# Second mixer of a two-block network: heads in pairs, keys in three stages, f32 sums

## The chip, the core and the metric

The program runs on one core of one Trainium2 chip. The metric is the device time of one execution in microseconds (us), the median of a few runs. The engines are called PE (TensorE), DVE (VectorE), ACT (ScalarE), POOL (GpSimd) and SP (SyncE, which issues the DMAs). PSUM has eight banks here, `ps0` to `ps7`, of 128 x 512 f32.

## What is computed

Ten stages on 512 tokens of width 1024: six of a first block (four gated FFNs, a recurrent mixer, a stick-breaking attention mixer) and four of a second block. The change touches only the stick-breaking mixer, the fifth stage:

```python
def stick_breaking_mixer(h, w_qkv, w_out):
    q, k, v = jnp.split(h @ w_qkv, 3, axis=-1)      # 16 heads of 64
    for s0 in range(0, seqlen, Q_BLOCK):
        end = s0 + Q_BLOCK
        ...
        z = jnp.einsum("bqhd,bkhd->bhqk", qb, kb).astype(jnp.float32) * scale
        mask = k_pos[None, :] < q_pos[:, None]
        log_1m = jnp.where(mask, jax.nn.log_sigmoid(-z), 0.0)
        between = lax.cumsum(log_1m, axis=3, reverse=True) - log_1m
        att = jnp.where(mask, jnp.exp(jax.nn.log_sigmoid(z) + between), 0.0)
        outs.append(jnp.einsum("bhqk,bkhd->bqhd", att.astype(vb.dtype), vb))
    ...
    return o @ w_out
```

With softplus(z) = -log_sigmoid(-z) this is att = exp(z - sum of softplus(z) over this key and all later ones), for keys before the query.

## The kernel before

**Layout.** Activations lie with features on partitions and the 512 tokens along the free axis. A weight block of 128 x 128 arrives by DMA in chunks of eight (`RAW`), is split by ACT into a rounded high half (`SPH`, type fp32r) and by DVE into the rest (`SPL`), and every projection is three fp32r matmuls per block (L740 to L742). Chunks are split a few ahead of PE (`halve_to`). Each engine runs its own list of instructions in the order in which it is written, with waits on counting semaphores; a planner (`Ring.plan`) gives each tile its PSUM bank and tells what must have ended before.

**The mixer** (`mix1` in each engine's program). Q and K are projected into `WK` units 0 to 7 and 8 to 15 (unit = 512 columns, two heads in one unit, head h on partitions 64*(h%2) up), V by tokens into units 16 to 23 (L780 to L782, copied out by ACT at L1586). Then 16 heads, one after the other. For a head the scores are made with keys on partitions, in four tiles of 128 keys, `kt` = 3, 2, 1, 0, with 512 - 128*kt queries each (128, 256, 384, 512 columns; 1280 in all):

- PE `scores` (L1095): four f32 matmuls with 64 rows, into PSUM.
- DVE `start_tile`: x = max(z, 0) (L2224), y = z - 2x (L2226); ACT: exp (L1604), ln(1 + .) (L1606); DVE `end_tile` (L2231): the negated softplus; POOL (L2605) zeroes the masked triangle with an affine select; ACT (L1611) rounds to fp32r (`LMH`), POOL (L2616) subtracts for the low half (`LML`).
- PE `weights` (L1111): for each key tile the suffix sum, as matmuls with a triangle (`SUF`) or `ONES` over this and all later tiles, once for the high and once for the low half, added onto the scores in PSUM: 2 x 2560 columns of fp32r a head.
- ACT (L1628): exp out of PSUM into `AT`; POOL (L2605) zeroes the triangle again.
- PE `values` (L1122): four f32 matmuls with 64 columns into bank `ob`, shared by two heads. ACT (L1634) and DVE (L2250) make the high and low half of the pair's output in `HH`, `HL`.

PE's order is `weights(h)`, `scores(h+1)`, `values(h)`. Then the output projection `project_out` (64 blocks; output tile m over its 8 inputs k, m after m), squares by ACT, copies and a running sum of squares by DVE (`squares_of_out`, `copies_of_out`), the sums over rows (L802, L804), a normalisation and the next stage.

Of the kernel before, what the change touches and what calls it, by code (L numbers as in the profile page):

```python
# [59 lines left out]
def constants():  # L60
# [16 lines left out]
    c["suffix"] = (i >= t)  # L77
    c["ones"] = np.ones((128, 128))
# [141 lines left out]
EARLY_OUT = {1: [4, 5, 6, 7]}  # L220
# [25 lines left out]
def build(nc, a, order, known):  # L246

    ctx = ExitStack()
    with ctx:
# [80 lines left out]
        def al(m):  # L330
            return AL[:, m * T:(m + 1) * T]
# [39 lines left out]
        def u8(x, rows=slice(0, 128), first=0, n=32):  # L371
# [5 lines left out]
        stick = {"LMH": [AL[:, u * T:u * T + 1280] for u in (3, 6)], "LML": [AL[:, u * T:u * T + 1280] for u in (9, 12)],  # L377
                 "AT": [WK[:, u * T:u * T + 1280] for u in (37, 40)]}
# [36 lines left out]
        def out_of(s):  # L415

            return Yh if s in NAMES or s in (CONV0, CONV1) else Y0 if s == MIX0 else Ya
# [162 lines left out]
        def plan_mix1():  # L580
            s = MIX1
            plan_first(s, "proj", lambda i: ("qk", i))
            ps.plan(("xsum", s), ("xln", s))
            ps.plan(("rcolp",), ("rcln",))
            for i in range(6, 16):
                ps.plan(("proj", s, i), ("qk", i))
                plan_chunk(BASE[s] + i)
            for half in range(2):
                for c in range(4):
                    ps.plan(("vp", s, half, c), ("v", half, c))  # L590

            def scores(h):
                for kt in (3, 1, 0):
                    ps.plan(("z", h, kt), ("att", h, 2 if kt == 3 else kt))
                for kt in (3, 1, 0):
                    scr.plan(("zx", h, kt), ("zl", h, 2 if kt == 3 else kt))
                    scr.plan(("zy", h, kt), ("lo", h, 2 if kt == 3 else kt))
            scores(0)
            for h in range(16):
                if h < 15:  # L600
                    scores(h + 1)
                if h % 2 == 0:
                    ps.plan(("ob", h // 2), ("al1", h // 2), hold=True)
                else:
                    ps.release(("ob", h // 2))
            plan_postnorm(s, BASE[s] + 24, 8)
# [105 lines left out]
        def tensor_program(e):  # L712
# [355 lines left out]
            def mix1(s):  # L1068
# [8 lines left out]
                for i in range(6, 16):  # L1077
                    project(s, i, "l1_w_qkv", cols[i])
                for half in range(2):
                    project_tokens(s, half, 512, "l1_w_qkv", 2048 + 512 * half)  # L1080
                off = [0, 512, 896, 1152]
                SO = al(21)[:, 0:256]
                SUF, ONES = SO[:, 0:128], SO[:, 128:256]

                def zof(h, kt):
                    b = ps["z", h, 3 if kt == 2 else kt]
                    return b[:, 256:384] if kt == 3 else b[:, 0:512 - 128 * kt]

                def scores(h):
                    m, p0 = h // 2, 64 * (h % 2)  # L1090
                    w.wait_ge(("qk", m), ("qk", 8 + m))
                    for kt in range(3, -1, -1):
                        if kt != 2:
                            w.wait_ge(*ps.before("z", h, kt))
                        e.matmul(zof(h, kt), wk(8 + m)[p0:p0 + 64, 128 * kt:128 * kt + 128],  # L1095
                                 wk(m)[p0:p0 + 64, 128 * kt:T], start=kt != 2, stop=False,
                                 skip_group_check=True).then_inc(pe_done.did(("z", h, kt)))

                def weights(h):
                    lh, ll = stick["LMH"][h % 2], stick["LML"][h % 2]  # L1100
                    w.wait_ge(("suf",))
                    for kt in range(3, -1, -1):
                        w.wait_ge(("lo", h, kt))
                        if kt == 3:
                            w.wait_ge(("zneg", h, 2))
                        for half in (lh, ll):
                            for jt in range(3, kt - 1, -1):
                                nj, oj = 512 - 128 * jt, off[jt]
                                sh = 128 * (jt - kt) + (256 if kt == 3 else 0)
                                b = ps["z", h, 3 if kt == 2 else kt]  # L1110
                                mm = e.matmul(b[:, sh:sh + nj], SUF if jt == kt else ONES, half[:, oj:oj + nj],  # L1111
                                              start=False, stop=half is ll and jt == kt, skip_group_check=True)
                        mm.then_inc(pe_done.did(("sum", h, kt)))

                def values(h):
                    p0, at = 64 * (h % 2), stick["AT"][h % 2]
                    if h % 2 == 0:
                        w.wait_ge(*ps.before("ob", h // 2))
                    w.wait_ge(("cut", h, 0), ("v", 1, 3))
                    for kt in range(4):  # L1120
                        n, o = 512 - 128 * kt, off[kt]
                        mm = e.matmul(ps["ob", h // 2][p0:p0 + 64, 128 * kt:T], wk(16 + 2 * kt, 2)[:, 64 * h:64 * h + 64],  # L1122
                                      at[:, o:o + n], start=kt == 0, stop=kt == 3, skip_group_check=True)
                    mm.then_inc(pe_done.did(("val", h)))
                scores(0)
                for h in range(16):
                    weights(h)
                    if h < 15:
                        scores(h + 1)
                    values(h)  # L1130
                project_out(s, "l1_w_out", 8, hp, lambda k: ("al1", k))
# [188 lines left out]
        def scalar_program(e):  # L1320
# [254 lines left out]
            def mix1(s):  # L1575
# [3 lines left out]
                rsqrt_of(ps["rcolp",][:, 0:4], rcol, EPS6, 1.0, ("rcln",), ("rcol",))  # L1579
                for i in range(6, 16):  # L1580
                    halve_to(ahead_of(s, i))
                for half in range(2):
# [5 lines left out]
                w.wait_ge(("sufl",))  # L1588
                e.activation(al(21)[:, 0:256], wk(24)[:, 0:256], ACT.Copy).then_inc(act_done.did(("suf",)))
                off = [0, 512, 896, 1152]  # L1590
                ln_exp_table()

                def zy(h, kt):
                    q = 256 if kt == 3 else 0
                    return scr["zy", h, 3 if kt == 2 else kt][:, q:q + 512 - 128 * kt]

                def zof(h, kt):
                    b = ps["z", h, 3 if kt == 2 else kt]
                    return b[:, 256:384] if kt == 3 else b[:, 0:512 - 128 * kt]

                def start_tile(h, kt):
                    y = zy(h, kt)
                    w.wait_ge(("zneg", h, kt))
                    e.activation(y, y, ACT.Exp).then_inc(act_done.did(("zexp", h, kt)))  # L1604
                    w.wait_ge(("zexp", h, kt))
# [1250 lines left out]
```

## Time and profile before

| | us |
|---|---|
| median of 3 runs | 3832.0 (3827.67 to 3833.7) |
| the profiled execution | 3837.11 |
| its span in the trace | 3835.4 |
| busy PE / DVE / ACT / POOL | 3588.8 / 1944.1 / 1399.8 / 99.8 |
| the mixer's heads in the trace, from the last V projection to the first matmul of the output projection | about 1725 to 1979.8 |

The page gives each engine's busy time, the 40 slices with the clock that PE was granted, and the chain of work that ended last. In the slices PE is at nine tenths almost everywhere at a granted clock of 0.9 to 1.0 of full speed, and in slices 19 and 20 the granted clock is 0.6 and 0.7, POOL is busy for the only time and the DMAs rest: that is the mixer. A full granted clock (1.00) is 2.4 GHz, 0.50 is 1.2 GHz. An f32 matmul stands in the trace as two records (one for each pass over the columns; together a column takes about four times as long as one of fp32r), an fp32r one as one. Rates are therefore read from the starts of matmuls that follow each other; the length of one record holds some 0.17 us until its result is seen.

### The profile page before, as it was taken

To read this page: it belongs to the slowest core of one execution; us is meant where nothing else is said; L and a number is where in the kernel's file an instruction comes from. 1 tells how busy PE (TensorE), PEld (TensorE's weight loads), DVE (VectorE), ACT (ScalarE), POOL (GpSimd) and SP (SyncE) were. 2 spreads that over 40 slices of the span, in tenths; PEclk is the share of its full clock that TensorE was granted. 3 is DMA by queue.
4 is the path that set the end of the run, shared out by engine and by line. 5 is a ranking of instruction groups with operands and counts; after the bars stand their busy time and mean duration, and the time that the engine had idled before them with its cause. 6 is when DMAs were issued, how large, how long until landed. Compare 5 with 4: busy or idle time off the path is not lost.

```text
span 3835.4 us, 47526 instructions
## 1 busy us (share of the span) xinstructions
PE 3588.8 (94%) x20316; PEld 2825.4 (74%) x20316; DVE 1944.1 (51%) x2753; ACT 1399.8 (36%) x2086; POOL 99.8 (3%) x210
## 2 busy tenths in 40 slices
PE   8999886899999999897889999999999999889998
PEld 6888665778887888784457888765788877668886
DVE  5554665356544643423436443646566344656652
ACT  4322453233323332325434322235444233444433
POOL 0000000000000000003320000000000000000000
PEclk9999986899999999996679999989999999899999
DMA  5444320024443432220002222310233231012231
GB/s 181 143 143 143 110 94 4 2 94 154 143 143 104 160 109 95 79 97 6 0 28 83 99 96 97 126 61 2 71 105 99 96 125 65 28 39 94 99 99 55
DMA packets 93091, 342.37 MB, mean 89 GB/s; under 512 B 10320, under 2 KB 10960, under 8 KB 92368
## 3 DMA queue, kind: packets, MB, share of 16 engines
q1 hardware_dynamic: 92880, 339.33, 26.5%
q8 instruction: 160, 2.62, 0.3%
q14 instruction: 51, 0.42, 0.0%
HBM read 337.20 MB, written 2.10 MB: 88 GB/s over the span
## 4 chain that ended last, share of the span: by engine, by line
PE 83%; ACT 7%; DVE 7%; issue 2%; POOL 2%; DMA 0%; SPq 0%; ACTq 0%; DVEq 0%
PE ps L740 20%; PE ps L741 20%; PE ps L742 20%; PE ps L757 3%; PE ps L758 3%; PE ps L761 3%; POOL AL L2616 1%; ACT WK L1778 1%; PE ps L1111 1%; PE ps L780 1%; PE ps L781 1%; PE ps L782 1%; PE ps L809 1%; ACT SPH L1330 1%; ACT L1334 1%
## 5 line engine op out<-in xcount | busy, mean ns | idle before, releaser
L1864 DVE TENSOR_TENSOR SPL<-RAW,SPH 128x1024 fp32r<-128x1024 f32 x522 | 637.1, 1224 | 1096.5 <-ACT SPH L1330 1096.4
L740 PE MATMUL ps<-HH,SPH 128*128 128x512 f32 x2416 | 959.5, 397 | 21.8 <-DVE WK L2207 7.7
L1330 ACT ACTIVATE SPH<-RAW 128x1024 fp32r<-128x1024 f32 x522 | 548.8, 1056 | 1103.2 <-PE ps L742 975.4
L741 PE MATMUL ps<-HL,SPH 128*128 128x512 f32 x2416 | 947.4, 392 | 0.0
L742 PE MATMUL ps<-HH,SPL 128*128 128x512 f32 x2416 | 946.5, 392 | 0.0
L740 PEld LDWEIGHTS ps<-HH,SPH 128*128 128x128 f32 x2416 | 458.5, 190 | 132.1 <-issue 12.5
L741 PEld LDWEIGHTS ps<-HL,SPH 128*128 128x128 f32 x2416 | 458.6, 190 | 97.6 <-issue 3.9
L742 PEld LDWEIGHTS ps<-HH,SPL 128*128 128x128 f32 x2416 | 457.9, 190 | 97.2
L740 PE MATMUL ps<-AH,SPH 128*128 128x512 f32 x1088 | 423.8, 390 | 0.0
L742 PE MATMUL ps<-AH,SPL 128*128 128x512 f32 x1088 | 423.3, 389 | 0.0
L741 PE MATMUL ps<-AL,SPH 128*128 128x512 f32 x1056 | 410.8, 389 | 0.0
L757 PE MATMUL ps<-HH,SPH 128*128 128x512 f32 x480 | 200.6, 418 | 55.2 <-ACT HH L1370 25.0
L742 PEld LDWEIGHTS ps<-AH,SPL 128*128 128x128 f32 x1088 | 204.2, 188 | 42.6
L740 PEld LDWEIGHTS ps<-AH,SPH 128*128 128x128 f32 x1088 | 204.3, 188 | 42.0
L741 PEld LDWEIGHTS ps<-AL,SPH 128*128 128x128 f32 x1056 | 198.3, 188 | 41.1
L758 PE MATMUL ps<-HH,SPL 128*128 128x512 f32 x480 | 197.9, 412 | 0.0
L757 PEld LDWEIGHTS ps<-HH,SPH 128*128 128x128 f32 x480 | 97.4, 203 | 83.6 <-ACT HH L1370 29.1
L761 PE MATMUL ps<-HL,SPH 128*128 128x512 f32 x480 | 122.2, 390 | 0.0
L1111 PE MATMUL ps<-AL 128*128 128x128 f32 (+2 forms) x320 | 77.3, 390 | 45.7 <-POOL AL L2616 45.6
L1392 ACT ACTIVATE SCR<-SCR 128x512 f32<-128x512 f32 x88 | 55.8, 634 | 169.3 <-DVE SCR L1935 169.3
L758 PEld LDWEIGHTS ps<-HH,SPL 128*128 128x128 f32 x480 | 97.6, 203 | 20.9
L1851 DVE SCALAR_TENSOR_TENSOR ADA<-RAW,PCT,ADA 128x1024 f32<-128x1024 f32 x84 | 107.4, 1279 | 0.0
(416 smaller groups left out, 3900.7 us busy)
## 6 DMA issues: line engine op xcount, KB each, us to landing
RAW<-in_ws SPq DMA_DIRECT2D x522, 512.0 KB, 3.3
RAW<-in_wa SPq DMA_DIRECT2D x96, 512.0 KB, 3.3
WK<-in_sm SPq DMA_DIRECT2D x2, 2784.0 KB, 9.7
WK<-in_cst SPq DMA_DIRECT2D x2, 1664.0 KB, 7.4
X<-in_x SPq DMA_DIRECT2D x8, 256.0 KB, 7.7
out<-X SPq DMA_DIRECT2D x8, 256.0 KB, 2.1
WK<-in_sm SPq DMA_DIRECT2D x1, 768.0 KB, 5.1
WK<-in_cst SPq DMA_DIRECT2D x3, 128.0 KB, 2.4
```

Source lines behind the costliest of these rows:

```text
L740: e.matmul(out, wh, rhs[0], start=start, stop=False)
L741: e.matmul(out, wh, rhs[1], start=False, stop=False)
L742: mm = e.matmul(out, wl, rhs[0], start=False, stop=stop)
L757: e.matmul(ps["proj", s, i][:], wh, hh, start=k == 0, stop=False)
L758: e.matmul(ps["proj", s, i][:], wl, hh, start=False, stop=False)
L761: mm = e.matmul(ps["proj", s, i][:], wh, hl, start=False, stop=k == 7)
L780: e.matmul(o, hh, wh[:, 0:n], start=k == 0, stop=False)
L1111: mm = e.matmul(b[:, sh:sh + nj], SUF if jt == kt else ONES, half[:, oj:oj + nj], start=False, stop=half is ll and jt == kt, skip_group_ch ...
L1330: e.activation(SPH[:, q:q + 1024], RAW[:, r:r + 1024], ACT.Copy).then_inc(hi_ready.did(("hi", n)))
L1392: e.activation(scr["g", s, m], scr["g", s, m], ACT.Silu).then_inc(act_done.did(("silu", s, m)))
L1851: e.scalar_tensor_tensor(ADA[:], raw, c, ADA[:], ALU.mult, ALU.add).then_inc(dve_done.did(("ada", i)))
L1864: e.tensor_tensor(SPL[:, q:q + 1024], RAW[:, r:r + 1024], SPH[:, q:q + 1024].bitcast(F32), ALU.subtract).then_inc(lo_ready.did(("lo", n)))
```

## The change

- Two heads go together (a pair, m = 0 to 7), and the keys of a pair go in three stages: `STAGES` 0: tiles kt 2 and 3 (384 columns a head in one bank), 1: kt 1 (384), 2: kt 0 (512). That is 24 steps n = 3m + stage. Each step has a bank for each head (`zs`, six banks, so three steps), outputs alternate over banks 6 and 7.
- PE writes the scores of the two heads alternately (partitions 0 to 63 and 64 to 127), and the values alternately (output partitions 0 to 63 and 64 to 127).
- The masks are added in PSUM: after the scores one fp32r matmul of 128 columns per key tile and head, identity times a triangle of -1e30 (`IR`, `CA`, made by ACT at the start of the mixer from a constant that is loaded with the others). POOL has nothing left to do in the mixer.
- Softplus is max(z, ln(1 + exp(min(z, 40)))): DVE min, ACT exp, ACT ln, DVE max, each on 384 or 512 columns of a head, in buffers `SP`.
- The suffix sums are f32 matmuls of `SP` itself (2560 columns a head, no halves), with negated triangle and ones. The order of keys within a step changes which of them are one matmul.
- PE's order is scores(n+2), sums(n), values(n-1). scores(0) stands ahead of the V projections.
- The pair's output goes over Q and K of that pair (`AH` units m and 8+m), the copies of the output projection over V (`Y1`).
- `EARLY_OUT` for this stage: output tiles 0 to 3 first take inputs 0 to 6, then input 7 for the four; then tiles 4 to 7 alike. The chunks are split up to other numbers ahead (`ahead_of_out`).

```diff
-EARLY_OUT = {1: [4, 5, 6, 7]}
+EARLY_OUT = {1: [4, 5, 6, 7], 4: [0, 1, 2, 3, 4, 5, 6]}
...
+        STAGES = [((2, 0), (3, 256)), ((1, 0),), ((0, 0),)]
+        WIDTH, AT_SP = [384, 384, 512], [0, 384, 768]
...
+            zs, outs = (0, 1, 4, 5, 2, 3), (6, 7)
+
+            def scores(n):
+                for h in range(2):
+                    ps.plan(("z", n, h), ("att", n, h), group=zs)
...
+                def scores(n):
+
+                    m, tiles = n // 3, STAGES[n % 3]
+                    w.wait_ge(("qk", m), ("qk", 8 + m), ("masks1",), *ps.before("z", n, 0), *ps.before("z", n, 1))
+                    for kt, o in tiles:
+                        for h in range(2):
+                            p0 = 64 * h
+                            e.matmul(ps["z", n, h][:, o:o + 512 - 128 * kt],
+                                     wk(8 + m)[p0:p0 + 64, 128 * kt:128 * kt + 128], wk(m)[p0:p0 + 64, 128 * kt:T],
+                                     start=o == 0, stop=False, skip_group_check=True)
+                    for kt, o in tiles:
+                        for h in range(2):
+                            mm = e.matmul(ps["z", n, h][:, o:o + 128], IR, CA, start=False, stop=False,
+                                          skip_group_check=True)
+                    mm.then_inc(pe_done.did(("z", n)))
...
+                    for h in range(2):
+                        z, sp = ps["z", n, h], SP[m % 2][h]
+                        w.wait_ge(("sp", n, h))
+                        e.matmul(z[:, 0:WIDTH[st]], SUF, sp[:, AT_SP[st]:AT_SP[st] + WIDTH[st]], start=False, stop=False,
+                                 skip_group_check=True)
...
+                        for x, o in later:
+                            mm = e.matmul(o, ONES, x, start=False, stop=True, skip_group_check=True)
+                        mm.then_inc(pe_done.did(("sum", n, h)))
...
+                scores(1)
+                for n in range(24):
+                    if 0 < n < 22:
+                        scores(n + 2)
+                    sums(n)
+                    if n == 0:
+                        scores(2)
+                    else:
+                        values(n - 1)
+                values(23)
+                project_out(s, "l1_w_out", 8, lambda k: (ah(k), ah(8 + k)), lambda k: ("al1", k))
...
+                def logs(n):
+                    for h in range(2):
+                        w.wait_ge(("min", n, h))
+                        e.activation(part(n, h), part(n, h), ACT.Exp).then_inc(act_done.did(("exp", n, h)))
+                    for h in range(2):
+                        w.wait_ge(("exp", n, h))
+                        e.activation(part(n, h), part(n, h), ACT.Ln, bias=ONE).then_inc(act_done.did(("ln", n, h)))
...
+                for n in range(24):
+                    if n == 0:
+                        weights(0)
+                    if n < 22:
+                        logs(n + 2)
+                    if n:
+                        weights(n)
+                    if n and n % 3 == 0:
+                        out_hi(n // 3 - 1)
...
+                low(0)
+                high(0)
                 halve_to(BASE[s] + 23 + AHEAD)
...
+                low(1)
+                for n in range(24):
+                    if n < 22:
+                        low(n + 2)
+                    if n < 23:
+                        high(n + 1)
+                    if n > 1 and n % 3 == 1:
+                        out_lo(n // 3 - 1)
+                out_lo(7)
```

**PE, one head before.** The list of PE between the scores of head 0 and the first sums of head 1 (`AL` holds the halves of the softplus, `WK` Q, K, V and the weights):

```order
L1111 MATMUL ps<-AL 128x128 [waits s_gpsimd_done]
L1111 MATMUL ps<-AL 128x256
L1111 MATMUL ps<-AL 128x384
L1111 MATMUL ps<-AL 128x512
L1111 MATMUL ps<-AL 128x128
L1111 MATMUL ps<-AL 128x256
L1111 MATMUL ps<-AL 128x384
L1111 MATMUL ps<-AL 128x512
L1095 MATMUL ps<-WK 128x128
L1095 MATMUL ps<-WK 128x256
L1095 MATMUL ps<-WK 128x384
L1095 MATMUL ps<-WK 128x512
```

The sums of each key tile wait for POOL; the scores of the next head come behind them.

**PE, one step now.** The same engine in the steps n = 2 and 3 (L1096 scores, L1101 masks, L1112 and L1122 sums, L1133 values):

```order
L1096 MATMUL ps<-WK 128x512 [waits s_scalar_done]
L1096 MATMUL ps<-WK 128x512
L1101 MATMUL ps<-AL 128x128 x2
L1112 MATMUL ps<-WK 128x384 [waits s_vector_done]
L1122 MATMUL ps<-WK 128x128
L1112 MATMUL ps<-WK 128x384 [waits s_vector_done]
L1122 MATMUL ps<-WK 128x128
L1133 MATMUL ps<-WK 64x512 x2
```

Scores moved two steps ahead of the sums that use them; what they wait for is now ACT, whose exponentials free the banks of the step before.

**ACT, one head before:**

```order
L1628 ACTIVATE WK<-ps 128x128 [waits s_tensor_done]
L1628 ACTIVATE WK<-ps 128x256
L1628 ACTIVATE WK<-ps 128x384 [waits s_tensor_done]
L1628 ACTIVATE WK<-ps 128x512 [waits s_tensor_done]
L1604 ACTIVATE SCR<-SCR 128x128 [waits s_vector_done]
L1606 ACTIVATE SCR<-SCR,SML 128x128 [waits s_scalar_done]
L1604 ACTIVATE SCR<-SCR 128x256 [waits s_vector_done]
L1606 ACTIVATE SCR<-SCR,SML 128x256 [waits s_scalar_done]
```

**ACT, two steps now** (L1614 exp, L1617 ln, L1622 the weights, L1627 the high half of a pair's output):

```order
L1614 ACTIVATE WK<-WK 128x512 [waits s_vector_done] x2
L1617 ACTIVATE WK<-WK,SML 128x512 [waits s_scalar_done] x2
L1622 ACTIVATE WK<-ps 128x384 [waits s_tensor_done] x2
L1627 ACTIVATE AH<-ps 128x512 [waits s_tensor_done]
L1614 ACTIVATE WK<-WK 128x384 [waits s_vector_done] x2
L1617 ACTIVATE WK<-WK,SML 128x384 [waits s_scalar_done] x2
L1622 ACTIVATE WK<-ps 128x384 [waits s_tensor_done] x2
```

The exponentials of a step now stand behind the logarithms of the step two further on; the rounding copies (L1611) are gone.

## Rows read from the trace of the kernel before

**Rows 1.** Stretch, length; busy us of PE, PEld, DVE, ACT, POOL; granted clock; DMA.

```profile
1900.00:1950.00 50.00, 43.23 (x113) 22.38 (x112) 21.18 (x44) 24.93 (x55) 19.11 (x39) 0.64 0.00 1
```

**Rows 2.** The chain that ended last, one head: start us, us, what.

```profile
1877.85 1.27 POOL AL L2616
1879.16 2.71 PE ps L1111 x8
...
1893.53 1.28 POOL AL L2616
```

**Rows 3.** Waits from 1733 to 1985 us: us in total, times, longest.

```profile
DVE SCR L2224 <- PE ps L1095: 99.9, 15, 9.1
...
PE ps L1111 <- POOL AL L2616: 45.6, 41, 6.9
```

**Rows 4.** The same mixer stretches finer, split where the granted clock changes.

```profile
1864.87:1875.11 10.24, 10.24 (x21) 4.64 (x19) 5.66 (x12) 5.23 (x11) 2.67 (x6) 0.50 0.00 1
1875.11:1878.52 3.41, 2.06 (x13) 1.57 (x12) 0.00 (x0) 1.92 (x5) 2.02 (x4) 1.00 0.00 0
```

**Rows 5.** PE in a later stage, 2641 to 2651 us: paired f32 matmuls and masks at clock 1.00.

```profile
2641.39 2.09 PE L1272 MATMUL ps<-WK 128*64 128x512 f32 x12
...
2644.37 1.13 PE L1244 MATMUL ps<-WK 64*128 64x512 f32 x4
2645.43 0.44 PE L1248 MATMUL ps<-AL 128*128 128x128 f32 x2
...
2647.27 1.14 PE L1244 MATMUL ps<-WK 64*128 64x384 f32 x8
2648.33 0.66 PE L1248 MATMUL ps<-AL 128*128 128x128 f32 x4
...
2650.00 0.70 PE L1244 MATMUL ps<-WK 64*128 64x256 f32 x4
2650.64 0.44 PE L1248 MATMUL ps<-AL 128*128 128x128 f32 x2
```

**Rows 6.** PE at the end of the output projection: last block, then f32 sums.

```profile
2023.67 0.39 PE L742 MATMUL ps<-HH,SPL 128*128 128x512 f32 x1
2023.90 1.02 PE L802 MATMUL ps<-ACC,CST 128*128 128x512 f32 x2
...
2024.76 1.12 PE L804 MATMUL ps<-SCR,CST 128*128 128x512 f32 x2
```

**Rows 7.** PE at clock 0.50: one f32 matmul of 512 columns, two records.

```profile
1884.53 1.91 PE L1095 MATMUL ps<-WK 64*128 64x512 f32 x2
```

**Rows 8.** Groups by line and shape, 1733 to 1985 us: busy us, mean ns of one.

```profile
L1606 ACT ACTIVATE SCR<-SCR,SML 128x512 f32<-128x512 f32 x16 | 11.6, 722 | 0.5
...
L1628 ACT ACTIVATE WK<-ps 128x384 f32<-128x384 f32 x16 | 7.9, 495 | 0.7 <-PE ps L1111 0.6
...
L2224 DVE TENSOR_SCALAR SCR<-ps 128x512 f32<-128x512 f32 x16 | 10.9, 684 | 0.0
...
L2224 DVE TENSOR_SCALAR SCR<-ps 128x384 f32<-128x384 f32 x15 | 8.3, 551 | 0.0
L1604 ACT ACTIVATE SCR<-SCR 128x384 f32<-128x384 f32 x15 | 7.9, 524 | 6.1 <-DVE SCR L2226 6.1
```

**Rows 9.** The chain again: four copies of V, and the first output matmul.

```profile
1726.25 2.31 ACT WK L1586 x4
...
1979.76 0.73 PE ps L740
```

**Rows 10.** The later stage again, by stretches, with PE's granted clock.

```profile
2640.00:2660.00 20.00, 18.55 (x121) 10.17 (x121) 15.21 (x40) 12.22 (x39) 0.00 (x0) 1.00 0.00 1
```

**Rows 11.** DVE in the last 5 us of the output projection: start us, us.

```profile
2019.29 0.69 DVE L1905 TENSOR_TENSOR ACC<-ACC,SCR 128x512 f32<-128x512 f32 x1 [3.02 <-ACT SCR L1356]
...
2019.89 0.69 DVE L1907 COPY Ya<-ps 128x512 f32<-128x512 f32 x1
...
2020.50 1.22 DVE L1864 TENSOR_TENSOR SPL<-RAW,SPH 128x1024 fp32r<-128x1024 f32 x1
```

More of the change, by code:

```diff
@@ L75, in constants @@
     c["diag"] = i32 == j32
-    c["suffix"] = (i >= t)
-    c["ones"] = np.ones((128, 128))
+    c["suffix"] = -1.0 * (i >= t)
+    c["ones"] = -np.ones((128, 128))
+    c["later"] = np.where(i < t, 0.0, -1e30)
     pm = np.zeros((128, 128))
@@ new lines, in values @@
+                def values(n):
+                    m, tiles = n // 3, STAGES[n % 3]
+                    if n % 3 == 0:
+                        w.wait_ge(*ps.before("ob", m))
+                    w.wait_ge(("att", n, 0), ("att", n, 1), ("v", 1, 3))
+                    for kt, o in tiles:
+                        for h in range(2):
+                            p0 = 64 * h
+                            mm = e.matmul(ps["ob", m][p0:p0 + 64, 128 * kt:T],
+                                          wk(16 + 2 * kt, 2)[:, 64 * (2 * m + h):64 * (2 * m + h) + 64],
+                                          AT[n % 4][h][:, o:o + 512 - 128 * kt], start=kt == 2, stop=kt == 0,
+                                          skip_group_check=True)
+                    mm.then_inc(pe_done.did(("val", n)))
@@ L1079, in mix1 @@
+                scores(0)
                 for half in range(2):
                     project_tokens(s, half, 512, "l1_w_qkv", 2048 + 512 * half)
[L1081 to L1131, printed above, removed]
+                scores(1)
+                for n in range(24):
+                    if 0 < n < 22:
+                        scores(n + 2)
+                    sums(n)
+                    if n == 0:
+                        scores(2)
+                    else:
+                        values(n - 1)
@@ L1631, in values @@
-                def values(h):
-                    if h % 2:
-                        w.wait_ge(("val", h), ("vp", s, 1, 3))
-                        e.activation(hp(h // 2)[0], ps["ob", h // 2][:], ACT.Copy).then_inc(
-                            act_done.did(("ah1", h // 2)))
-                scores(0)
-                for h in range(16):
-                    weights(h)
-                    if h < 15:
-                        scores(h + 1)
-                    values(h)
+                logs(1)
@@ L2243, in mix1, with part @@
[L2243 to L2251 removed]
+                SP = stick["SP"]
+                def part(n, h):
+                    o = AT_SP[n % 3]
+                    return SP[n // 3 % 2][h][:, o:o + WIDTH[n % 3]]
@@ new lines, in low, with high @@
+                def low(n):
+                    w.wait_ge(("z", n))
+                    for h in range(2):
+                        w.wait_ge(*([("sum", n - 4 - n % 3, h)] if n >= 6 else ah_free(s)))
+                        e.tensor_scalar(part(n, h), ps["z", n, h][:, 0:WIDTH[n % 3]], 40.0, None, ALU.min).then_inc(
+                            dve_done.did(("min", n, h)))
+                def high(n):
+                    for h in range(2):
+                        w.wait_ge(("ln", n, h))
+                        e.tensor_tensor(part(n, h), ps["z", n, h][:, 0:WIDTH[n % 3]], part(n, h), ALU.max).then_inc(
+                            dve_done.did(("sp", n, h)))
```

180 lines of the change are left out of this document (49 added, 131 removed).

## The prediction

> **What bounds the kernel now.** I read the slices first: PE is busy nearly everywhere and the clock is full nearly everywhere, except in the mixer. So the mixer is where time can come from, and the rest (projections at one fp32r matmul after the other) is untouched by the change. Then the mixer by stretches: in 50 us PE is "busy" 43.2, but at a granted clock of 0.64 [rows 1]. The chain shows who ends last: from one head's last POOL subtraction to the next head's is 1893.53 - 1877.85 = 15.7 us, and it runs through all engines: POOL's halves, PE's sums behind them, PE's next scores, DVE, ACT, POOL again [rows 2]. 16 heads of 15.7 are 251 us; with the start the mixer takes from about 1725, where the V projections end and ACT copies their last tiles, to 1979.8, where the output projection begins [rows 9]: 254.8 us. The waits say the same: DVE waits 9.1 us at most in a head, 99.9 in all, for the scores, because they stand behind the sums in PE's list, and PE waits 45.6 us for POOL's low halves [rows 3]. No engine has enough work for 15.7 us at full speed; the loop is a chain handed round. Its pauses also cost clock: after a stretch at 1.00 in which PE was busy 2.06 of 3.41 us the clock is at 0.50 again, where the sums, scores and values then run without a pause (10.24 of 10.24 us busy) at half rate [rows 4].
>
> **PE's work for a pair now, at the full clock.** The nearest rows for scores, masks and values are those of a later stage, which pairs its heads in the same way [rows 5].
> - Scores and masks, from the first matmul to the result in PSUM. A 512-column pair takes 2645.43 - 2644.37 = 1.06, two masks 0.44: 1.50 for stage 2. A 256-column pair takes 0.64, so 128 columns are 0.21, and 384 with two masks is 0.85 + 0.44 = 1.29 (stage 1). Stage 0, 256 and 128 with four masks, is 1.06 (for 384 and 128) - 0.21 + 0.66 = 1.51. PE is free again some 0.17 earlier each time: 4.3 us to the results, 3.8 of PE.
> - Sums: f32 of 512 columns start 0.86 apart [rows 6], 1.68 ns a column. 2 x 512, 2 x 768 and 2 x 1280 columns are 1.72, 2.58 and 4.30: 8.6 us. That is the part that gets dearer, twice what 2 x 2 x 2560 fp32r columns would cost at the same clock.
> - Values: 2.09 for 512, 384 and 128 columns, less the 0.17, and about 0.5 for 256: 2.4.
>
> Together 14.8 us a pair, against 2 x 15.7 = 31.4 now. By rows 5 a 512-column f32 pair costs 1.06 where two alone would cost 2 x 0.86, so pairing gives 1.6 times, not 2. The Trainium skill (TensorEngine Tiling (Array Packing), Theoretical Speedup and Key Properties) has up to 2 times for 64 rows, and says that changing the tiling mode drains the engine. By the 2 the scores would be 2.15 instead of 2.7 and the values 2.15 instead of 2.4, by its drain rule something in between; this case's trace has both effects in 1.06, and the sum goes by that.
>
> **ACT's work.** One exp, ln of 512 or exp out of PSUM of 384 takes 0.63 to 0.72 and 0.50 [rows 8], but four in a row of 512 take 2.31 [rows 9], 0.58 each; with 0.107 us less for 128 columns less (the 0.524 of the shorter exp) a queued one of 384 is 0.47. DVE takes 0.68 or 0.55 a tile [rows 8], and has four a step, 7.5 us a pair with the output: never the bound. POOL's affine selects and subtractions, the rounding copies and two of three DVE passes leave the chain.
>
> **The new loop, step by step.** PE's scores(n+2) wait for both exponentials of step n-1, since these free the banks. Behind them come: first min on DVE, two exps and two lns of step n+2, then two exps of step n, which free the next banks. Two paths compete:
> - by ACT: scores to result + one DVE tile + 4 ACT + 2 ACT + about 0.2 for ends and semaphores. n = 3m: 1.50 + 0.68 + 4 x 0.58 + 2 x 0.47 + 0.2 = 5.64. n = 3m+1: 1.51 + 0.55 + 6 x 0.47 + 0.2 = 5.08. n = 3m+2: 1.29 + 0.55 + 4 x 0.47 + 2 x 0.58 + 0.2 = 5.08.
> - by PE: scores + sums + 0.2 + one exp. n = 3m: 1.33 + 1.72 + 0.7 = 3.75. n = 3m+1: 1.34 + 2.58 + 0.7 = 4.62. n = 3m+2: 1.12 + 4.30 + 0.17 + 0.6 + 0.05 = 6.24.
>
> Values(n-1) go into the time in which PE waits for the exponentials. The later end counts: 5.64 + 5.08 + 6.24 = 17.0 us a pair, of which PE works 14.8. If every ACT tile takes its full single length the first two steps are 0.4 longer each: 17.8.
>
> **Start and end.** scores(0) now stand ahead of the V projections and wait for the last Q/K tile to leave bank 1 (about 1.0), and take 1.5: +2.6 with nothing beside them. Their logarithms are hidden by the V projections. After V, ACT first splits a chunk and copies the last V tiles (to +3.5 as now [rows 9]), then does two exps, two lns and the exponentials of step 0: step 1 begins at +6.4. Steps 1 and 2: 11.3. Steps 3 to 20: six pairs of 17.0, 102. From step 21: scores, sums and values 3.05 + 1.0, sums(22) and values to 7.3, sums(23) 4.30, last exp 0.8, last values 1.0: 13.5. Total 2.6 + 6.4 + 11.3 + 102 + 13.5 = 135.8 us in place of 254.8: **-119.0**.
>
> The other order of the output projection costs nothing at its start (inputs 0 to 6 are long there, banks 0 to 5 free). At its end it does: output tiles 4 to 7 end 3 matmuls of 0.227 apart, 0.68 us [rows 6], instead of 24, 5.4. Behind tile 4 stand on DVE: sum, copy, a chunk to split (1.22), sum, copy, sum at 0.6 each, where now all but one are over before the last matmul [rows 11]. DVE's last sum then comes about 3 us after PE's last matmul, where L802 now follows at once [rows 6]: **+3**. Bounds: 0, if the chunk is split earlier, and 5. ACT's mask constants, a table load and the longer DMA cost nothing: they lie beside projections.
>
> Sum: -116. For the clock I add 2 (below): -114. On the profiled execution's span 3835.4 - 114 = 3721; it lay 5 us above the median with what surrounds it, so against the median 3832.0: **3718 us**.
>
> **Rivals.**
> - *The clock still falls, once in most pairs.* In a step 3m PE pauses 5.64 - 1.33 - 1.72 - 1.0 = 1.6 us, in 3m+1 0.5. Before, a pause of 1.35 us between short bursts was followed by the low level [rows 4]; in the later stage PE is busy 18.55 of 20 us in small pieces and keeps 1.00 [rows 10]. With 1.6 in 17 us I expect it to hold, so I add only 2 us. Falling once a pair for 10.24 us [rows 4] doubles 5 us of PE work, of which the pauses take 1 to 2: 4 us a pair, 32 in all: 3750. Chance 0.21. The Trainium skill (TensorE: Matmul & The Clock Gate, Part 1) calls the low clock the default that activity lifts; by that rule a denser loop lifts itself, and the trace agrees, since the fully busy low stretch of rows 4 is followed by 1.00.
> - *The heads of a pair don't overlap*, in the sums' neighbourhood unlike in rows 5. Scores 4.3 instead of 2.7, values 4.3 instead of 2.4, a third hidden: +2.5 a pair, 20 us: 3738. Chance 0.05. Against it: same partitions and same form of instruction as in rows 5.
> - *PE at the low level for the whole mixer.* PE alone then sets the loop: 2 x 14.8 = 29.6 a pair, 237 and 12 for the ends, near 250: with the +3 no change, 3830. Chance 0.02.
> - *Slower: the same, and f32 weight loads show.* At 0.50 one f32 matmul of 512 is 1.71 between starts [rows 7], double; a pair has 36 passes of sums, many of only 128 or 256 columns, each with its own load of weights. If each shows 0.1 us of its load, a pair takes 33.2 us, the mixer 278 with its ends: +26, 3858. It decides from 31.4 - 29.6 = 1.8 us a pair, 0.05 a pass, and only without the full clock. Chance 0.03. Against it: PE would then be busy without pause, the very stretch that rows 4 show ended by 1.00.
>
> **Numbers.** Forecast 0.69: 3706 to 3728 (start and end 4 either way, 17.0 to 17.8 a pair). The range takes in the falling clock with its bounds (2 to 6 us a pair) and the serial pairs, and leaves out the last two: 3706 to 3766. A measurement of this kernel can tell about 0.2% from no change, 7.7 us. Faster 0.95, within 0.2% 0.02, slower 0.03.
>
> **What would show it.** Granted clock 1.00 in the mixer, PE about 87% busy; the scores of two heads starting together; from one pair to the next 17 us; ACT's wait for PE longest before the exponentials of stage 2, PE's wait for ACT longest ahead of the scores in steps 3m; POOL empty; L802 3 us behind the last matmul of the projection. I am wrong if a pair takes over 19 us at clock 1.00 (then an ACT or DVE tile or the sums are mis-sized), or if the clock is under 0.9.

## The result, and the profile after

The changed kernel takes 3720.4 us (median of 4 runs, 3719.26 to 3726.31), the kernel before 3829.8 (4 runs, 3824.83 to 3833.7): a ratio of 0.9718, 95% interval 0.9701 to 0.9735, 109.5 us less. The forecast was 3718, and 3706 to 3766 as its range.

In the following table the mixer stage is cut at the starts of PE's matmuls, in the two profiled executions. "Mixer" alone means, here and below, the part from the last V matmul to the first output-projection matmul.

| part of the mixer stage | before, us | after, us | difference |
|---|---|---|---|
| Q and K projections, now with scores(0) at their end | 65.3 | 67.0 | +1.7 |
| V projections | 43.3 | 47.8 | +4.5 |
| last V matmul to first output-projection matmul | 255.0 | 134.7 | -120.3 |
| output projection to L802 / L809 | 44.2 | 46.7 | +2.5 |
| from there to the next stage's first matmul | 7.0 | 8.6 | +1.6 |
| sum (of the unrounded parts) | 414.8 | 304.8 | -109.9 |

The sum agrees with the medians. The spans themselves differ by more (3835.4 and 3718.1): 4.8 us of that lie ahead of this stage and 2.6 behind it, in code that is the same in both. Where a kernel reaches this stage moves by more than that: in the 13 profiles of the changed kernel and its variants the V projections begin between 1669.5 and 1681.9 us. The kernel before, measured again beside the experiments, has medians of 3833.8, 3828.5 and 3825.9. Therefore the experiments below are read by this table first, and a difference of some 4 us between medians is not put down to an edit.

The whole mixer before and then 60 us of it after (columns as in [rows 1]):

```profile
1724.71:1979.69 254.98, 208.19 (x579) 115.23 (x577) 96.60 (x200) 123.86 (x270) 96.41 (x192) 0.65 0.01 3
```

```profile
1735.00:1795.00 60.00, 55.77 (x272) 33.36 (x270) 24.39 (x46) 33.98 (x69) 0.00 (x0) 1.00 0.00 0
```

The waits of the changed kernel from 1735 to 1860 us (us in total, times, longest):

```profile
DVE WK L2226 <- PE ps L1101: 67.9, 20, 4.7
ACT WK L1614 <- DVE WK L2226: 42.0, 20, 2.4
PEld ps L1096 <- ACT WK L1622: 19.3, 20, 2.2
ACT WK L1622 <- PE ps L1122: 14.1, 10, 2.7
...
PE ps L1096 <- ACT WK L1622: 7.9, 6, 1.3
```

The granted clock is 1.00 where its mean was 0.65, and POOL is empty. The 0.65 means that about 176 of the 255 us ran at the low level. PE's waits for POOL [rows 3] are replaced by one wait a pair of 1.3 us: the scores wait for ACT's exponentials of the step before. PE is busy 92% of the mixer. One pair on PE (start us, us):

```profile
1789.85 0.44 PE L1101 MATMUL ps<-AL 128*128 128x128 f32 x2
1790.12 1.07 PE L1112 MATMUL ps<-WK 128*128 128x512 f32 x2
1791.03 1.46 PE L1122 MATMUL ps<-WK 128*128 128x384 f32 x6
...
1794.58 0.87 PE L1133 MATMUL ps<-WK 128*64 128x384 f32 x4
1795.43 1.13 PE L1096 MATMUL ps<-WK 64*128 64x512 f32 x4
...
1798.64 1.08 PE L1133 MATMUL ps<-WK 128*64 128x512 f32 x4
1801.04 0.92 PE L1096 MATMUL ps<-WK 64*128 64x256 f32 x8 [1.31 <-ACT WK L1622]
...
1805.13 0.87 PE L1133 MATMUL ps<-WK 128*64 128x256 f32 x8
1806.07 0.92 PE L1096 MATMUL ps<-WK 64*128 64x384 f32 x4
```

The scores of the steps begin at 1795.43, 1801.04 and 1806.07, and those of the step before the first of these at 1789.00: 6.43, 5.61 and 5.03 us for n = 3m+2, 3m and 3m+1, 17.07 a pair. The idle time in brackets stands only ahead of the scores that follow a step 3m.

### The profile page after: what moved, and what is told of

It is laid out like the page before. It is cut to its first block, busy times and chain, and to the rows that moved or that the text cites. A ratio compares the mean times of both kernels' runs of the same rounds, so it can differ in the third digit from the quotient of the medians.

```text
span 3718.1 us, 47147 instructions
## 1 busy us (share of the span) xinstructions
PE 3504.7 (94%) x20348; PEld 2780.3 (75%) x20348; DVE 1902.6 (51%) x2657; ACT 1354.9 (36%) x1975; POOL 3.6 (0%) x18
## 4 chain that ended last, share of the span: by engine, by line
PE 86%; ACT 6%; DVE 5%; issue 1%; DMA 0%; SPq 0%; ACTq 0%; DVEq 0%
PE ps L747 21%; PE ps L749 20%; PE ps L748 20%; PE ps L764 3%; PE ps L765 3%; PE ps L768 3%; ACT WK L1784 1%; PE ps L787 1%; PE ps L788 1%; PE ps L789 1%; PE ps L816 1%; ACT SPH L1350 1%; PE ps L1122 1%; ACT L1354 1%; DVE SPL L1870 1%
## 5 line engine op out<-in xcount | busy, mean ns | idle before, releaser
L747 PE MATMUL ps<-HH,SPH 128*128 128x512 f32 x2352 | 933.6, 397 | 22.1 <-DVE WK L2213 8.1
L748 PE MATMUL ps<-HL,SPH 128*128 128x512 f32 x2352 | 922.3, 392 | 0.0
L749 PE MATMUL ps<-HH,SPL 128*128 128x512 f32 x2352 | 921.6, 392 | 0.0
L747 PEld LDWEIGHTS ps<-HH,SPH 128*128 128x128 f32 x2352 | 446.1, 190 | 129.2 <-issue 12.1
L748 PEld LDWEIGHTS ps<-HL,SPH 128*128 128x128 f32 x2352 | 446.0, 190 | 95.9 <-issue 3.9
L749 PEld LDWEIGHTS ps<-HH,SPL 128*128 128x128 f32 x2352 | 445.7, 189 | 94.1
L747 PE MATMUL ps<-AH,SPH 128*128 128x512 f32 x1152 | 448.9, 390 | 0.0
L749 PE MATMUL ps<-AH,SPL 128*128 128x512 f32 x1152 | 448.2, 389 | 0.0
L764 PE MATMUL ps<-HH,SPH 128*128 128x512 f32 x480 | 200.9, 419 | 55.0 <-ACT HH L1390 24.9
L747 PEld LDWEIGHTS ps<-AH,SPH 128*128 128x128 f32 x1152 | 216.2, 188 | 45.7 <-issue 0.8
L749 PEld LDWEIGHTS ps<-AH,SPL 128*128 128x128 f32 x1152 | 216.2, 188 | 45.0
L765 PE MATMUL ps<-HH,SPL 128*128 128x512 f32 x480 | 198.8, 414 | 0.0
L764 PEld LDWEIGHTS ps<-HH,SPH 128*128 128x128 f32 x480 | 97.6, 203 | 84.3 <-ACT HH L1390 29.8
L768 PE MATMUL ps<-HL,SPH 128*128 128x512 f32 x480 | 122.6, 391 | 0.0
L765 PEld LDWEIGHTS ps<-HH,SPL 128*128 128x128 f32 x480 | 97.7, 204 | 21.0
L768 PEld LDWEIGHTS ps<-HL,SPH 128*128 128x128 f32 x480 | 91.2, 190 | 19.5
```

Source lines behind the costliest of these rows:

```text
L747: e.matmul(out, wh, rhs[0], start=start, stop=False)
L748: e.matmul(out, wh, rhs[1], start=False, stop=False)
L749: mm = e.matmul(out, wl, rhs[0], start=False, stop=stop)
L764: e.matmul(ps["proj", s, i][:], wh, hh, start=k == 0, stop=False)
L765: e.matmul(ps["proj", s, i][:], wl, hh, start=False, stop=False)
L768: mm = e.matmul(ps["proj", s, i][:], wh, hl, start=False, stop=k == 7)
```

## Experiments

Each is an edit of the changed kernel, whose mixer takes 134.7 us.

### The order of the output projection

```diff
-EARLY_OUT = {1: [4, 5, 6, 7], 4: [0, 1, 2, 3, 4, 5, 6]}
+EARLY_OUT = {1: [4, 5, 6, 7]}
```

> The changed kernel, but the output projection of this mixer takes its tiles m one after the other again (EARLY_OUT without stage 4). My theory: the interleaved order costs at its end, since four output tiles finish 0.7 us apart and DVE and ACT still have three of them to do; the last sum over rows then comes 2.5 us late and runs at the low clock after the pause. Expected 4 us less than the changed kernel's 3720.4: 3716, with L809's counterpart right behind the last matmul and both sums at full clock. Rival: the end is hidden by the next stage's first loads, or the order helps at the start of the projection: 3720 or more.

Measured: 3712.0 us, ratio to the kernel before 0.9684 (0.967 to 0.9698). The two last parts of the table are 43.7 and 7.0 instead of 46.7 and 8.6: -4.7 us. The median moved by 8.4; 4.1 us of that lie ahead of this stage, where the code is the same. The end of the projection in the changed kernel:

```profile
1906.85 0.68 DVE L1911 TENSOR_TENSOR ACC<-ACC,SCR 128x512 f32<-128x512 f32 x1
...
1907.59 1.87 PE L809 MATMUL ps<-ACC,CST 128*128 128x512 f32 x2 [2.91 <-DVE ACC L1911]
1909.25 1.91 PE L811 MATMUL ps<-SCR,CST 128*128 128x512 f32 x2
```

and in this one:

```profile
1900.17 0.39 PE L749 MATMUL ps<-AH,SPL 128*128 128x512 f32 x1
1900.40 1.02 PE L809 MATMUL ps<-ACC,CST 128*128 128x512 f32 x2
```

PE's 2.91 us of waiting are DVE's sums of squares of the tiles that ended together. The two f32 sums then run at half rate (1.66 us apart in place of 0.86), where the granted clock behind the pause is the low one: the projection is 3.0 us longer than with the tiles in order, which is the wait, and the part behind it 1.6 us longer, which is the clock.

The wait is certain and the low clock behind it is not. Nine of the profiles have this pause of 2.91 us, and in three of them (V copies first, fp32r sums, no masks) the clock stayed at 1.00 while the two sums ran, and the part behind the pause took 7.0 us as without it. V copies first:

```profile
1895.07 1.13 PE L809 MATMUL ps<-ACC,CST 128*128 128x512 f32 x2 [2.91 <-DVE ACC L1913]
1896.03 1.02 PE L811 MATMUL ps<-SCR,CST 128*128 128x512 f32 x2
```

### The pause between the halves of V

```diff
-                    halve_to(BASE[s] + 16 + 4 * half + 3 + AHEAD)
+                    halve_to(BASE[s] + 16 + 4 * half + 2 + AHEAD)
                     for c in range(4):
+                        if c == 2:
+                            halve_to(BASE[s] + 16 + 4 * half + 3 + AHEAD)
```

> The changed kernel, but ACT copies two V tiles of each half before it splits the chunk that it can only split when the half is over. Theory: PE's pause of 2.6 us between the halves of the V projection, followed by a stretch at the low clock, is the wait for the PSUM banks 2 and 3, which the second half now takes over from the first and ACT frees behind its split. Expected: the pause shrinks below 1 us, the clock stays, 4 us less: 3716. Rival: PE waits for DVE's split of that chunk, as the profile's releaser says; then the split comes 1.2 us later and the time is 3721 or 3722.

Measured: 3716.4 us, 0.97 (0.9683 to 0.9717). The median moved by 4, and its four runs spread over 14 us (3708.8 to 3722.9), so it shows nothing by itself; the trace is clearer: V projections 43.4 us instead of 47.8, the other parts up to L809 within 0.4 us. (The last part was 7.0 instead of 8.6, though the edit leaves its code as it was: the sums ran at the full clock, as shown above. That is not counted for the edit.) The pause in the changed kernel, on ACT and on PE, and the clock around it (1.00, then 0.50):

```profile
1700.44 1.06 ACT L1350 ACTIVATE SPH<-RAW 128x1024 fp32r<-128x1024 f32 x1 [4.38 <-PE ps L789]
1701.40 2.40 ACT L1635 ACTIVATE WK<-ps,SML 128x512 f32<-128x512 f32 x4
...
1702.90 0.64 PE L787 MATMUL ps<-SPH,HH 128*128 128x512 f32 x1 [2.56 <-DVE SPL L1870]
```

```profile
1700.00:1703.04 3.04, 0.48 (x3) 0.17 (x2) 1.23 (x1) 2.60 (x4) 0.00 (x0) 1.00 0.00 1
1703.04:1706.46 3.42, 3.42 (x9) 2.65 (x10) 0.00 (x0) 0.76 (x2) 0.00 (x0) 0.50 0.52 157
```

and after the edit:

```profile
1690.65 1.37 ACT L1637 ACTIVATE WK<-ps,SML 128x512 f32<-128x512 f32 x2 [2.28 <-PE ps L789]
1692.75 1.06 ACT L1350 ACTIVATE SPH<-RAW 128x1024 fp32r<-128x1024 f32 x1 [0.73 <-PE ps L789]
...
1693.84 1.23 DVE L1872 TENSOR_TENSOR SPL<-RAW,SPH 128x1024 fp32r<-128x1024 f32 x1 [4.21 <-ACT SPH L1350]
```

The releaser named in the profile, DVE's split, was not what PE waited for. It ended 0.1 us behind the second V copy, by which PE got its banks back; with the copies in front the split comes as late behind the half as before, and the pause is gone. Of the 4.5 us some 2.8 are the wait and 1.6 the low clock: with the two heads apart (next section) the same pause of 2.56 us is followed by a clock of 1.00, and the V projections take 46.2 us.

### Two heads apart

The loops over heads and over the scores and masks are swapped:

```diff
-                    for kt, o in tiles:
-                        for h in range(2):
+                    for h in range(2):
+                        for kt, o in tiles:
                             ...
-                    for kt, o in tiles:
-                        for h in range(2):
+                        for kt, o in tiles:
                             mm = e.matmul(ps["z", n, h][:, o:o + 128], IR, CA, start=False, stop=False,
```

> The changed kernel, but PE writes all scores and masks of one head and then those of the other, so that no two score matmuls of different heads stand next to each other. Theory: the overlap of two 64-row matmuls is worth about 1.6 us of scores a pair, three more changes between forms cost 0.1 to 0.2 each, and scores lie in every step's path: 2.0 to 2.4 us a pair, 16 to 19 in all: 3738. Rival (the heads gain nothing by standing side by side, the gain is all in order and masks): 3720 to 3723.

Measured: 3752.4 us, 0.979 (0.9774 to 0.9805); the mixer 165.9 us, 31.2 more. That is 1.7 times what was expected. Scores and masks of 384 columns in this kernel and, in a second place, of 512:

```profile
1802.15 0.91 PE L1096 MATMUL ps<-WK 64*128 64x384 f32 x2
1802.99 0.33 PE L1100 MATMUL ps<-AL 128*128 128x128 f32 x1
1803.25 0.91 PE L1096 MATMUL ps<-WK 64*128 64x384 f32 x2
...
1851.36 1.09 PE L1096 MATMUL ps<-WK 64*128 64x512 f32 x2
1852.38 0.33 PE L1100 MATMUL ps<-AL 128*128 128x128 f32 x1
```

and the stretch (columns as before):

```profile
1735.00:1885.00 150.00, 141.88 (x550) 81.01 (x548) 48.08 (x89) 66.43 (x131) 0.00 (x0) 0.95 0.00 0
```

One head's 384 columns take 0.84 us (1802.15 to 1802.99), as much as both heads' side by side in the changed kernel, 0.85 to the first mask at 1789.85:

```profile
1789.00 0.92 PE L1096 MATMUL ps<-WK 64*128 64x384 f32 x4
```

One head's 512 columns take 1.02 (1851.36 to 1852.38), both heads' 1.06 (1795.43 to 1796.49 in the changed kernel). Beside each other the second head is nearly free. A mask that stands alone between two score matmuls takes 0.26 us (1802.99 to 1803.25), where two together take 0.27 (1789.85 to 1790.12). And 20.5 us of the mixer ran at the low clock, which had been there for none. The 31.2 us can be divided: at full clock the steps take 7.4, 6.8 and 6.0 us, 20.15 a pair instead of 17.07, so 3.1 us a pair are work, 1.4 times the 2.0 to 2.4 expected. By these steps some 22 of the 31.2 us are work and some 9 the low clock (an estimate).

### Scores one step ahead

```diff
-                    if 0 < n < 22:
-                        scores(n + 2)
+                    if n < 23:
+                        scores(n + 1)
                     sums(n)
...
-                    if n < 22:
-                        logs(n + 2)
-                    if n:
-                        weights(n)
+                    if n < 23:
+                        logs(n + 1)
+                    weights(n)
```

and alike on DVE.

> The changed kernel with scores one step ahead instead of two (PE: scores(n+1), sums(n), values(n-1); ACT: logs(n+1), weights(n); DVE: min and max of n+1). Theory: what holds steps 3m and 3m+1 is that scores two ahead need banks that ACT frees only behind the logarithms; one ahead they need none of that, the softplus of a step (some 5 us from its scores) fits beside the sums and values of the step before, and PE's own 15 us a pair become the bound: 15 to 15.7 us a pair in place of 17.1, 3705 to 3710. Rival (the two steps of lead carry the gain): PE waits for the softplus in every step, 1 to 3 us, and the clock falls: 19 to 24 us a pair, 3736 to 3775.

Measured: 3709.7 us, 0.9676 (0.9661 to 0.969); the mixer 124.3 us, 10.4 less. PE is busy in 60.00 of 60 us:

```profile
1735.00:1795.00 60.00, 60.00 (x297) 35.44 (x295) 28.10 (x50) 37.42 (x75) 0.00 (x0) 1.00 0.00 1
```

A pair takes 15.50 us, as expected. The two steps of lead are not what the gain comes from; with this order of ACT they cost 10 us.

### Where DVE's time counts: min twice, max twice

```diff
+                        e.tensor_scalar(part(n, h), ps["z", n, h][:, 0:WIDTH[n % 3]], 40.0, None, ALU.min).then_inc(
+                            dve_done.did(("min0", n, h)))
+                        w.wait_ge(("min0", n, h))
                         e.tensor_scalar(part(n, h), ps["z", n, h][:, 0:WIDTH[n % 3]], 40.0, None, ALU.min).then_inc(
                             dve_done.did(("min", n, h)))
```

> The changed kernel with every min pass on DVE done twice. Theory: in steps 3m and 3m+1 the path scores, min, exp, ln, weights sets the step, so the second head's exp comes 1.35 and 1.1 us later and so does the next step; step 3m+2 is set by PE and hides it. 2.45 us a pair, 20 in all: 3740. Rival (PE, busy 93% of the mixer, is the bound in all steps): 3720 to 3722.

Measured: 3743.2 us, 0.9774 (0.975 to 0.9797); the mixer 159.4 us, 24.7 more, 23.9 us of it at the low clock. At full clock the steps 3m and 3m+1 take 7.06 and 6.22 us instead of 5.61 and 5.03, 2.6 us a pair more (2.45 expected), and the step 3m+2 takes 6.43 as before. The low clock makes four of the steps 3m+1 longer (7.2, 8.2, 8.0 and 7.9 us instead of 6.2), 6.4 us in all; the other 18.3 are the path.

The same with the max pass:

> The changed kernel with every max pass on DVE done twice: the same added work as in the run with the min passes, but at a place where the result is needed only a step later. Theory: DVE is busy two fifths of the mixer, nothing waits: 3720 to 3722. Rival (DVE's load as such, or its reads of PSUM, slow the loop): about 3740.

Measured: 3716.5 us, 0.9709 (0.9688 to 0.9729); the mixer 135.4 us, 0.7 more. 48 passes more in both kernels: before exp they cost 18 us and 6 more by the clock, behind ln 1. With the min twice, ACT waits for DVE and PE for ACT:

```profile
ACT WK L1614 <- DVE WK L2229: 70.9, 41, 3.6
...
PE ps L1096 <- ACT WK L1622: 21.0, 10, 2.8
```

### Sums at a quarter of the cost

DVE's max writes fp32r (below), and ACT makes triangle and ones in fp32r:

```diff
-                        e.tensor_tensor(part(n, h), ps["z", n, h][:, 0:WIDTH[n % 3]], part(n, h), ALU.max).then_inc(
+                        o = AT_SP[n % 3]
+                        e.tensor_tensor(stick["SPR"][n // 3 % 2][h][:, o:o + WIDTH[n % 3]],
+                                        ps["z", n, h][:, 0:WIDTH[n % 3]], part(n, h), ALU.max).then_inc(
```

> The changed kernel with the suffix sums in fp32r from the softplus rounded once, without a low half: the sums take a quarter of the columns' time, but their precision is that of the high half alone. PE's work of a pair falls from about 15 to 8.5 us. Theory: two of three steps are set by ACT, so at full clock only step 3m+2 gets shorter, by 1.2 us: 15.8 us a pair, 3710; but PE then pauses half of the time, and if the clock falls for it, the scores in every step's path take twice as long: 19 to 20 us a pair, 3740. I expect the second. Rival (PE is the bound in all steps): 10 to 11 us a pair, 3670.

Measured: 3712.9 us, 0.97 (0.968 to 0.9721); the mixer 132.4 us, 2.3 less.

```profile
1735.00:1855.00 120.00, 91.45 (x416) 58.50 (x417) 48.77 (x90) 65.65 (x132) 0.00 (x0) 0.79 0.00 0
```

61.4 us of the mixer run at the low clock. PE's saved work became pauses of up to 2.5 us and work at the low clock. The expectation chose 3740, and that did not come: the low clock did not hold throughout. Towards the end of the mixer, pairs of 17.8 and 16.3 us alternate, 17.07 in the mean, which is just what a pair takes with the f32 sums.

### Without masks

The mask matmuls are left out.

> The changed kernel without the mask matmuls (keys after the query are left in, so this part of the computation is left out). Theory: masks lie in every step's path between scores and min: 0.37, 0.58 and 0.37 us, 1.3 a pair: 10 us less, 3710. Rival (they lie beside ACT's work): 3718 to 3720.

Measured: 3713.4 us, 0.9694 (0.967 to 0.9718); the mixer 127.0 us, 7.7 less. From one pair to the next it takes 15.9 us instead of 17.07: the steps 3m and 3m+1 are shorter by 0.37 and 0.59, which is what was expected of the masks there (0.37 and 0.58), and the step 3m+2 by 0.22. The masks are in the path of all three.

### The other way out of the wait, and all together

With two steps of lead, ACT does the exponentials first:

```diff
-                    if n == 0:
-                        weights(0)
+                    weights(n)
                     if n < 22:
                         logs(n + 2)
-                    if n:
-                        weights(n)
```

> The changed kernel, scores two steps ahead as there, but ACT does the exponentials of step n before the logarithms of step n+2. The run with scores one ahead gave 124.3 us from the V projections to the output projection instead of 134.7, with PE nearly without a wait. Theory: what cost the 10 us was not the lead itself but that the exponentials, which free the banks, stood behind the logarithms; with them in front PE waits under 0.5 us a step, 15.5 us a pair, mixer 124 to 126 us, 3709 to 3712. Rival (three steps' banks and two steps of lead cannot go together at any order of ACT): 133 to 135 us, 3720.

Measured: 3706.9 us, 0.9692 (0.9673 to 0.9711); the mixer 125.4 us, 9.3 less, PE busy in 60 of 60 us. So the lead and three steps' banks go together well; it was ACT's order.

The first, second and fourth edit in one kernel, f32 sums as in the change:

> The three single edits together: output tiles in order, V copies ahead of the split, scores one step ahead; f32 sums. Theory: they lie in different places, so from the changed kernel's segments -4.7 - 4.5 - 10.4 = -19.6 us (the second edit's 1.6 in the tail is in the first's): 3701. Rival (they share a cause, the clock): 3705 to 3710.

Measured: 3699.7 us, 0.9671 (0.9657 to 0.9686). Parts: 67.0, 43.4, 123.9, 43.7, 7.0, in all 284.9, 20.0 less than the changed kernel's.

The same with fp32r sums:

> The same with the sums in fp32r from the softplus rounded once (no low half). With two steps of lead this had gained 2.3 us, since PE waited for ACT and 61 us ran at the low clock. Theory: with one step ahead PE's 8.5 us a pair and ACT's 11 us are both under what the chain scores, min, exp, ln, max, sums, exp needs; ACT becomes the bound at 11.5 to 13 us a pair if the clock holds: mixer 95 to 106 us, 3673 to 3684. If it falls, scores at half rate still hide behind ACT: 110 us, 3690. Rival (PE's pauses cost as much as its work saves): 3700, no better than with f32 sums.

Measured: 3665.4 us, 0.9583 (0.956 to 0.9606); the mixer 87.1 us, 3.4 of it at the low clock, and 10.7 us a pair.

And with two steps of lead and the exponentials first:

> fp32r sums, output tiles in order, V copies first, scores two steps ahead with ACT's exponentials in front of the logarithms. Theory: two steps of lead hide the softplus chain wholly, ACT with 11 us a pair is the bound, 11.5 us a pair at full clock: mixer 95 us, 3673; at most 3 us from the run with one step of lead. Rival: the exponentials in front make ACT wait for PE's sums in each step, 13 to 14 us a pair, mixer 110 us, 3690.

Measured: 3650.7 us, 0.9543 (0.9529 to 0.9558); the mixer 79.1 us at full clock throughout, 8.0 less than with one step of lead, where at most 3 were expected. So with the short sums the second step of lead is worth something. Both kernels are faster than expected, since a pair takes less than ACT's 11 us by single durations; from one step 3m to the next here, on PE and on ACT:

```profile
1762.14 0.92 PE L1098 MATMUL ps<-WK 64*128 64x256 f32 x8
...
1765.47 0.92 PE L1098 MATMUL ps<-WK 64*128 64x384 f32 x4 [0.21 <-ACT WK L1625]
...
1768.80 1.13 PE L1098 MATMUL ps<-WK 64*128 64x512 f32 x4
...
1771.81 0.49 PE L1098 MATMUL ps<-WK 64*128 64x256 f32 x2
```

```profile
1761.71 1.15 ACT L1617 ACTIVATE WK<-WK 128x512 f32<-128x512 f32 x2
...
1771.38 1.15 ACT L1617 ACTIVATE WK<-WK 128x512 f32<-128x512 f32 x2
```

9.7 us a pair, with one pause of 0.27 us on ACT and one of 0.21 on PE. Both engines are full; which of them sets the pair was not separated. This is the fastest kernel of the study; its sums take the softplus rounded to fp32r where the changed kernel sums it in f32, and it is 49 us below `e10_all_f32`, the fastest with f32 sums.

## Why the prediction was right

**The loop.** A pair was summed to 5.64 + 5.08 + 6.24 = 17.0 us and measured 5.61 + 5.03 + 6.43 = 17.07. Two of three steps go by ACT's path and one by PE. The run with min twice against max twice shows it: the longer min makes the steps 3m and 3m+1 longer and leaves the step 3m+2 at 6.43, and the longer max changes none. The two runs that take ACT's logarithms out of the way of its exponentials end PE's wait. The first two steps came out to 0.05 us because queued ACT instructions were taken at their spacing in [rows 9] and not at their length in [rows 8].

**PE's work.** This was summed too low: 14.8 us a pair, where it is 15.5 with PE never waiting (one step ahead 15.50, exponentials first 15.55). Scores and masks came out (1.33, 1.35 and 1.12 to PE's next work); the sums take 1.88, 2.74 and 4.46 us instead of 1.72, 2.58 and 4.30, 0.16 more in each step, and the values about 2.7 instead of 2.4. The step 3m+2, where PE never rests, was 6.43 instead of 6.24 for this reason: 0.16 for the sums and 0.03 for the values, which took 0.85 us beside an exponential that the sum had at 0.82.

The error hardly shows in the time, and that is luck. PE's work in a step 3m+1 is 4.90 us (exponentials first) and ACT's path 5.03, so the pause of 0.5 us that the prediction had there was all but filled; a little more work on PE and this step would have gone by PE too. PE was busy 92% of the mixer and not the 87% of the prediction's signs. The mixer from the last V matmul was summed to 133.2 and measured 134.7.

**The overlap of heads.** The times of a pair were right, since they came from rows of the same form. The factor of 1.6 was not: it set 1.06 against twice 0.86, the spacing of 128-row matmuls that follow their like. One 64-row matmul of 512 columns between masks takes 1.02 us, so that two side by side save nearly one of the two. This is why the heads apart cost 31 us and not the 16 to 19 that were expected, together with the low clock that the expectation left out.

**The clock.** With PE busy 92% of the mixer the clock was 1.00 throughout. The rule that the prediction cites from the Trainium skill (TensorE: Matmul & The Clock Gate, Part 1), that activity lifts the clock, agrees with this. The rival that was given 0.21 did not come, but it stands close by. One min pass more a head and step brought 23.9 us of low clock, scores apart 20.5, fp32r sums 61.4. Its price of 4 us for each 10.24 us at the low clock was too high for the one run that shows it: with the min twice 23.9 us cost 6.4, 2.7 for 10.24. The allowance of 2 us was near in size (the clock cost 1.6 in each of two places) and wrong in place: the clock fell in the V projections and in the tail, behind pauses of 2.6 and 2.9 us.

**Start and end.** scores(0): +2.6 expected, +1.7 measured. Projection's order: +3 expected, +2.5 measured and +1.6 behind it at the low clock; the single edit gives back 4.7. What was missed is the reuse of banks 2 and 3 between the halves of V: the step "their logarithms are hidden by the V projections" looked at the engines and not at the banks that scores(0) holds meanwhile. It cost 4.5 us. The change was over-estimated by about as much (114 forecast, 109.9 by the table), since the other errors nearly cancel: -0.9 for scores(0), +1.3 for the mixer's difference, +1.1 for the projection's end with what follows it, -2 for the allowance. That the forecast of the time itself is 2.4 us off is helped by the kernel before, whose median over more runs is 2.2 lower.

**What stays open.** No run tells how the 120 us of the mixer divide between the shorter chain, the pairs and the clock. The mixer before ran 176 of its 255 us at the low clock; the runs here undo the pairing of scores and the masks one at a time, and none puts the old order of PE or POOL's work back.

## What to carry to other kernels

Write the loop as paths between the instruction that frees a bank and the next that needs it, one for each engine, with queued instructions at their spacing; the longest path of each step is the step. When a pipeline looks one step further ahead, put the instructions that free buffers in front of those that only work ahead, or the lead costs more than it brings. The pauses of PE of 2.6 and 2.9 us mostly cost twice here, as the wait and as 1.6 us of what followed at half the clock; price such a pause as the wait, with the clock as a likely addition. Work taken from PE is worth little until the wait beside it goes too (fp32r sums: 2.3 us alone, 36.8 with the order mended).

## What the runs showed of the hardware

- Two f32 matmuls of 64 rows on different halves of the partitions took 0.85 us together for 384 columns, and one alone 0.84; for 512 columns 1.06 and 1.02.
- A wait for several semaphores was put down in the profile to DVE's split, which ended within 0.1 us of the true releaser, an ACT copy; only the edit told them apart.
- ACT's queued exps and lns on 384 and 512 columns kept a spacing at which 18 tiles and one copy of a pair took 9.7 us, where their single lengths ([rows 8]) sum to about 11.
- The same pause of PE was followed by the low clock in some kernels and not in others: the one of 2.56 us between the halves of V in eight of nine profiles, the one of 2.91 us ahead of L809 in six of nine.
- In the changed kernel's mixer PE waited 1.3 us in one step of three and the granted clock stayed at 1.00; with the min pass twice, waits of up to 2.8 us (10 of them for ACT from 1735 to 1880 us, 21.0 us in all) stood in a mixer that spent 24 of its 159 us at the low clock.
